# First HGRN tile loaded, turned and given its levels between retention's pieces, in the memory of tokens already projected

## What is computed

```python
def step(state, inp):                     # retention
    scores = jnp.einsum('bqhd,bkhd->bhqk', qc, kc) * decay
    intra = jnp.einsum('bhqk,bkhe->bqhe', scores, vc)
    cross = jnp.einsum('bqhd,bhde->bqhe', qc, state) * q_decay[None, :, :, None]
...
def step(state, inp):                     # HGRN2
    b = jnp.cumsum(lfc, axis=1)
    diff = b[:, :, None] - b[:, None, :]
    w = jnp.where(causal[None, :, :, None, None], jnp.exp(jnp.minimum(diff, 0.0)), 0.0)
    attn = jnp.einsum('bihd,bjhd,bijhd->bhij', qc, kc, w)
    intra = jnp.einsum('bhij,bjhe->bihe', attn, vc)
    cross = jnp.einsum('bihd,bhde->bihe', qc * jnp.exp(b), state)
```

## Time and profile before

| | |
|---|---|
| median of 3 runs | 3606.19 us (3604.67 to 3606.43) |
| profiled execution | 3605.24 us, span 3603.1 us |
| PE busy | 3480.9 us, 97% |
| DVE busy | 2816.3 us, 78% |
| mean granted clock of TensorE | 0.981 |

### The profile page before, as it was taken

How to read it: one execution, slowest core, us unless ns; L and a number is a source line. 1 busy time by engine, 2 the same in 40 slices (tenths; PEclk the granted TensorE clock), 3 DMA queues, 4 the chain that set the end, 5 groups by cost and what they waited for, 6 DMA issues and landing times.

```text
span 3603.1 us, 71005 instructions
## 1 busy us (share of the span) xinstructions
PE 3480.9 (97%) x27042; PEld 2525.5 (70%) x27042; DVE 2816.3 (78%) x5663; ACT 1266.9 (35%) x3545; POOL 520.6 (14%) x798
## 2 busy tenths in 40 slices
PE   7999999999999997999999999999999999989998
PEld 6887888888864565555578878887888445555554
DVE  4666678647988998999955766884598799989996
ACT  3422333334431122444453133333344212234443
POOL 0110000100010355000000000001000115620000
PEclk9999999999999997999999999999999999979999
DMA  7443121322234335233432132214323333433332
GB/s 249 153 160 110 61 80 52 113 87 83 77 106 128 118 115 180 90 107 123 138 123 78 72 99 67 74 49 129 95 72 115 95 111 121 143 137 107 106 114 83
DMA packets 248304, 389.39 MB, mean 108 GB/s; under 512 B 30592, under 2 KB 176224, under 8 KB 247840
## 3 DMA queue, kind: packets, MB, share of 16 engines
q1 hardware_dynamic: 178560, 230.04, 20.6%
q0 software_dynamic: 39968, 122.30, 9.0%
q10 hardware_dynamic: 29440, 32.51, 2.9%
HBM read 264.42 MB, written 122.25 MB: 107 GB/s over the span
## 4 chain that ended last, share of the span: by engine, by line
PE 85%; DVE 10%; issue 2%; DMA 1%; ACT 1%; SPq 0%; DVEq 0%; POOL 0%; ACTq 0%; POOLq 0%
PE ps L1257 35%; PE ps L1665 14%; PE ps L1305 9%; PE ps L1448 5%; PE ps L1430 4%; PE ps L1417 3%; PE ps L1421 2%; PE ps L1618 2%; DVE e_t L2410 2%; PE ps L1580 2%; PE ps L1377 1%; PE ps L1483 1%; PE ps L1643 1%; PE ps L1232 1%; PE ps L1317 1%
## 5 line engine op out<-in xcount | busy, mean ns | idle before, releaser
L1257 PE MATMUL ps<-w_sb,s_t 128*128 128x256 f32 x3456 | 825.8, 382 | 7.4 <-DVE s_t L2337 3.7
L1257 PEld LDWEIGHTS ps<-w_sb,s_t 128*128 128x128 f32 x3456 | 628.0, 190 | 95.3 <-issue 13.0
L1257 PE MATMUL ps<-w_sb,hT 128*128 128x256 f32 x2592 | 635.2, 384 | 5.0 <-ACT hT L1816 2.3
L1665 PE MATMUL ps<-wo_sb,mT 128*128 128x512 f32 x1152 | 536.7, 606 | 2.6 <-ACT mT L2069 2.6
L1305 PE MATMUL ps<-w_sb,hT 128*128 128x512 f32 x1152 | 528.0, 601 | 0.5 <-issue 0.5
L1257 PEld LDWEIGHTS ps<-w_sb,hT 128*128 128x128 f32 x2592 | 473.5, 191 | 74.7 <-issue 11.8
L2315 DVE TENSOR_TENSOR row_t<-ps,p_t 128x256 f32<-128x256 f32 x324 | 136.9, 422 | 349.9 <-PE ps L1257 348.5
L1305 PEld LDWEIGHTS ps<-w_sb,hT 128*128 128x128 f32 x1152 | 207.8, 190 | 213.5 <-issue 209.0
L1665 PEld LDWEIGHTS ps<-wo_sb,mT 128*128 128x128 f32 x1152 | 206.8, 191 | 208.1 <-issue 197.8
L1056 POOL DMA_DIRECT2D projected<-row_t x216 | 117.9, 546 | 1441.4 <-DVE row_t L2400 865.6
L1839 ACT ACTIVATE p_t<-ps 128x256 f32<-128x256 f32 x324 | 124.0, 383 | 534.8 <-PE ps L1257 532.4
(11 more groups left out here) (266 smaller groups left out, 5801.9 us busy)
## 6 DMA issues: line engine op xcount, KB each, us to landing
projected<-row_t POOLq DMA_DIRECT2D x288, 256.0 KB, 2.5
w_sb<-in_w_in ACTq DMA_DIRECT2D x40, 512.0 KB, 5.1
hg_raw<-projected SPq DMA_DIRECT2D x72, 256.0 KB, 4.2
out_streams<-y_t POOLq DMA_DIRECT2D x36, 512.0 KB, 4.8
wa<-in_w_ada SPq DMA_DIRECT2D x10, 1536.0 KB, 7.3
hg_braw<-projected SPq DMA_DIRECT2D x108, 128.0 KB, 2.4
hg_raw<-projected SPq DMA_DIRECT2D x36, 384.0 KB, 3.3
mx_t<-mixed SPq DMA_DIRECT2D x36, 384.0 KB, 5.8
```

What stands on the lines that cost most here:

```text
L1257: mm = nc.tensor.matmul(ps[:, (u.run + k) % 2, 0:HB], x[:, c], w_blk[:, at[w], c * HB:(c + 1) * HB], start=opens and c == 0, stop=(c == KH ...
L1665: mm = nc.tensor.matmul(ps[:, 6 + g, :], mT[:, t % 2, k, :], wo_sb[:, k, g * GRP:(g + 1) * GRP], start=(k == 0), stop=(k == KC - 1))
```

## The change

`hT` is laid out by tiles (`[P, NT, KC, P]`), the tile t at place `NT - 1 - t`, so that the tiles that are projected first lie at its start. HGRN's buffers are cut out of one tensor over the same memory, with the buffers of even tiles in the first half and those of odd tiles in the second. The first half is free once piece (7, 9) is through; SP and POOL wait for that (`hg_room` and its like), SP in slot 19, POOL in slot 20, and then load tile 0 of HGRN and the tables, and clear `hg_d`. PE turns the decays, the queries and the keys of tile 0 in slots 21, 22 and 23, into PSUM bank 2, which `turn_ret` uses too: it waits for `ret.xT_ready` before, and the next `turn_ret` for `bank_taken`. ACT takes them in the same slots. DVE makes one level in each of slots 24 to 30, after all else in the slot, and the edges and keys in slot 31. Tile 1 is loaded, turned and taken where it was.

Left out below are the same change of the index of `hT` at five other places, and unchanged lines.

```diff
@@ -192,6 +192,11 @@
+def place_of(t):
...
+    return NT - 1 - t
@@ -215,6 +220,10 @@
+TURN_AT = 21
+LEVEL_AT = 24
+HG_PARTS = ("decays", "x", "keys")
@@ -371,11 +380,10 @@
-TURN_BANKS, O_BANK = (0, 1), 2
...
-HT_END = KC * NT * P
+TURN_BANKS, O_BANK, RET_BANK = (0, 1), 2, 2
...
+PLACE_N = KC * NT * P
 BLOCKS_AT = 18104
-HG_CORE = 14 * GW + P + 2 * P + 4 * GW + 4 + 12 * P + 16 * P + 8 * LEVELS * P + 8 * P + 128 + (SLOTS + 1) * 64
@@ -460,9 +468,9 @@
     with ExitStack() as s:
-        hT = sb(s, "hT", [P, KC, NT * P])
...
-        wa_early = hT[:, :, :].rearrange("p k n -> p (k n)").rearrange("p (c k n) -> p c k n", k=KC, n=3 * P)
+        hT = sb(s, "hT", [P, NT, KC, P])
...
+        wa_early = hT[:, :, :, :].rearrange("p t k n -> p (t k n)").rearrange("p (c k n) -> p c k n", k=KC, n=3 * P)
@@ -546,20 +554,33 @@
     with ExitStack() as s:
-        hg.raw = sb(s, "hg_raw", [P, 2, 7 * GW])
-        past = sb(s, "past", [P, P])
-        hg.sf = sb(s, "hg_sf", [P, 2, P])
-        hg.ed = sb(s, "hg_ed", [P, 2, GW])
-        hg.kd = sb(s, "hg_kd", [P, 2, GW])
-        hg.total = sb(s, "hg_total", [P, 2, 2])
-        hg.xT = sb(s, "hg_xT", [P, 2, 6, P])
-        hg.d = sb(s, "hg_d", [P, 2, 4, 2 * P])
-        hg.q = sb(s, "hg_q", [P, 2, LEVELS, 2, P])
-        hg.k = sb(s, "hg_k", [P, 2, LEVELS, 2, P])
-        hg.qx = sb(s, "hg_qx", [P, 2, 2, 2, P])
-        hg.tc = sb(s, "hg_tc", [P, 2, 64])
-        keep = sb(s, "keep", [P, SLOTS + 1, 64])
-        sb(s, "w_sb_first", [P, HT_END + KC * GRP - HG_CORE])
+        core = sb(s, "hg_core", [P, 2, PLACE_N // 2])
...
+        def both(at, *dims):
+            part = core[:, :, at:at + int(np.prod(dims))]
+            if len(dims) == 1:
+                return part
+            if len(dims) == 2:
+                return part.rearrange("p b (x n) -> p b x n", n=dims[1])
+            return part.rearrange("p b (x y n) -> p b x y n", y=dims[1], n=dims[2])
...
+        def single(at, n):
+            return core[:, 0, at:at + n]
...
+        hg.raw = both(0, 7 * GW)
+        hg.ed = both(7 * GW, GW)
+        hg.kd = both(8 * GW, GW)
+        hg.xT = both(9 * GW, 6, P)
+        hg.d = both(12 * GW, 4, 2 * P)
+        hg.q = both(16 * GW, LEVELS, 2, P)
+        hg.k = both(23 * GW, LEVELS, 2, P)
+        hg.qx = both(30 * GW, 2, 2, P)
+        hg.total = both(32 * GW, 2)
+        past = single(32 * GW + 8, P)
+        hg.sf = single(32 * GW + 8 + P, 2 * P).rearrange("p (c n) -> p c n", c=2)
+        hg.tc = single(32 * GW + 8 + 3 * P, P).rearrange("p (h n) -> p h n", h=2)
+        keep = single(32 * GW + 8 + 4 * P, (SLOTS + 1) * 64).rearrange("p (s n) -> p s n", n=64)
+        sb(s, "w_sb_first", [P, KC * GRP])
@@ -659,6 +680,9 @@
+    def turn_bank(key):
+        return RET_BANK if key[1] == 0 and key[0] in HG_PARTS else TURN_BANKS[TURNS[(0,) + key] % 2]
@@ -932,6 +956,9 @@
+            def hg_room(eng):
+                eng.wait_ge(proj_done, PIECES[l, 7, place_of(PLACE_N // 2 // D_MODEL - 1)].run + 1)
@@ -978,17 +1005,19 @@
                     load_ret_values(m - FORE + 1)
+                if m == TURN_AT - 2:
+                    hg_room(sp)
+                    load_hg_keys(0)
+                    load_hg_values(0)
+                    sp.dma_start(past[:, :], cols("after")).then_inc(hg.s_in, 16)
+                    sp.dma_start(keep[:, :, :].rearrange("p s n -> p (s n)"), cols("keep")).then_inc(hg.s_in, 16)
+                    for g, src in enumerate(state_ap(st_hgrn, l, 0)):
+                        sp.dma_start(hg.sf[:, 1, g * HD:(g + 1) * HD], src).then_inc(hg.s_in, 16)
...
                     sp.wait_ge(proj_done, last.run + 1)
-                    load_hg_keys(0)
-                    sp.dma_start(past[:, :], cols("after")).then_inc(hg.s_in, 16)
-                    sp.dma_start(keep[:, :, :].rearrange("p s n -> p (s n)"), cols("keep")).then_inc(hg.s_in, 16)
                     load_hg_keys(1)
-                    load_hg_values(0)
                     load_hg_values(1)
-                    for g, src in enumerate(state_ap(st_hgrn, l, 0)):
-                        sp.dma_start(hg.sf[:, 1, g * HD:(g + 1) * HD], src).then_inc(hg.s_in, 16)
@@ -1183,8 +1212,10 @@
                     store_piece(*REST_AT[m - 1])
+                if m == TURN_AT - 1:
+                    pool.wait_ge(proj_done, PIECES[l, 7, place_of(PLACE_N // 2 // D_MODEL - 1)].run + 1)
+                    clear_decays(0)
                 if m == REST_END + 1:
-                    clear_decays(0)
@@ -1302,7 +1333,7 @@
                     for k in range(KC):
-                        mm = nc.tensor.matmul(ps[:, p.bank, :], hT[:, k, t * P:(t + 1) * P], w_sb[:, g % 2, k, :],
+                        mm = nc.tensor.matmul(ps[:, p.bank, :], hT[:, place_of(t), k, :], w_sb[:, g % 2, k, :],
@@ -1516,6 +1547,9 @@
                     pe.wait_ge(ret.bs_ready, l * NT + NT - 1)
+                part = j + FORE - 3 - TURN_AT
+                if 0 <= part < len(HG_PARTS):
+                    pe.wait_ge(bank_taken, TURNS[l, HG_PARTS[part], 0] + 1)
@@ -1572,20 +1606,28 @@
                 n = TURNS[(l,) + key]
-                bank = TURN_BANKS[n % 2]
-                need(pe, bank_taken, n - 1)
+                bank = turn_bank(key)
+                need(pe, bank_taken, n if key[1] == 0 and key[0] in HG_PARTS else n - 1)
...
-            def turn_hg(t):
+            def turn_decays(t):
...
+            def turn_queries(t):
...
+                x = hg.raw[:, t % 2]
...
+            def turn_hg(t):
+                turn_decays(t)
+                turn_queries(t)
@@ -1697,13 +1739,18 @@
                 fill(2 * (more and m > 0))
-                if m == REST_END + 1:
+                if 0 <= m - TURN_AT < len(HG_PARTS):
+                    pe.wait_ge(ret.xT_ready, l * NT + j + 3)
+                if m == TURN_AT:
+                    turn_decays(0)
+                if m == TURN_AT + 1:
+                    turn_queries(0)
+                if m == TURN_AT + 2:
                     pe.wait_ge(hg.s_in, 64 * (l + 1))
+                    turn_keys(0)
+                if m == REST_END + 2:
...
                         bank_out(pe, PIECES[(l,) + PLAIN_ORDER["rest"][-n]])
-                    turn_hg(0)
-                    turn_keys(0)
-                if m == REST_END + 2:
@@ -2043,7 +2090,7 @@
                 act.wait_ge(bank_turned, n + 1)
-                return ps[:, TURN_BANKS[n % 2], :]
+                return ps[:, turn_bank(key), :]
@@ -2131,10 +2178,16 @@
                     bounds_ln(*REST_AT[m])
-                if m in (REST_END + 1, REST_END + 2):
-                    take_decays(m - REST_END - 1)
-                    take_x(m - REST_END - 1)
-                    take_keys(m - REST_END - 1)
+                if m == TURN_AT:
+                    take_decays(0)
+                if m == TURN_AT + 1:
+                    take_x(0)
+                if m == TURN_AT + 2:
+                    take_keys(0)
+                if m == REST_END + 2:
+                    take_decays(1)
+                    take_x(1)
+                    take_keys(1)
@@ -2883,11 +2936,9 @@
                     nc.vector.memset(hg.sf[:, 0, :], 0.0).then_inc(hg.clear, 1)
-                    for lv in range(0, 4):
-                        level_hg(0, lv)
-                if m == REST_END + 2:
-                    for lv in range(4, LEVELS):
-                        level_hg(0, lv)
+                if 0 <= m - LEVEL_AT < LEVELS:
+                    level_hg(0, m - LEVEL_AT)
+                if m == LEVEL_AT + LEVELS:
...
                 if m == BACK_SLOTS - 1:
```

More of the change, by code:

```diff
@@ L1263, in own @@
                     def own(t, kh):
-                        return hT[:, kh * KH:(kh + 1) * KH, t * P:(t + 1) * P]
+                        return hT[:, place_of(t), kh * KH:(kh + 1) * KH, :]
                     new = i == 0
@@ L1815, in modulated @@
                 for k in range(0, 4):
-                    last = nc.scalar.activation(hT[:, k, t * P:(t + 1) * P], ps[:, 2 + 2 * b, k * P:(k + 1) * P],
+                    last = nc.scalar.activation(hT[:, place_of(t), k, :], ps[:, 2 + 2 * b, k * P:(k + 1) * P],
                                                 ACT.Identity, scale=mod[:, d, KC + k, c:c + 1], bias=mod[:, d, k, c:c + 1])
@@ L2294, in modulated @@
                 for k in range(4, KC):
-                    last = nc.vector.tensor_scalar(hT[:, k, t * P:(t + 1) * P], ps[:, 3 + 2 * b, (k - 4) * P:(k - 3) * P],
+                    last = nc.vector.tensor_scalar(hT[:, place_of(t), k, :], ps[:, 3 + 2 * b, (k - 4) * P:(k - 3) * P],
                                                    mod[:, d, KC + k, c:c + 1], mod[:, d, k, c:c + 1], ALU.mult, ALU.add)
```

## The result

The changed kernel takes 3623.51 us (median of 4 runs, 3621.96 to 3626.11) against 3606.31 for the kernel before (4 runs, 3604.67 to 3607.93). The recorded ratio is 1.0050, with a 95% interval of 1.0038 to 1.0063; the two medians alone give 1.0048. It is slower by 17.2 us. The forecast was 3608, the range ended at 3621.

A forecast was written before the change was run, and what follows sets the result against it. PE was taken to bound the slots with pieces; after slot 31 PE and DVE take turns. Per layer +2.9 + 9 - 11 = +0.9, two layers +1.8: 3608 us, range 3590 to 3621.

The forecast's parts named there:

- an exchange: Whole kernel: what DVE loses to the pieces it gets back in the tail; 3608 us, chance 40%.
- Places in memory, POOL's clearing, SP's loads: New index of `hT`, `hg_d` clearing in slot 20, seven transfers thirteen slots earlier: claimed to cost nothing on the path.
- PE and ACT, slots 21 to 23: PE's turns of tile 0 where PE is full, +1.9, and waiting for ACT's copy, +1.0: +2.9 us a layer.
- DVE, slots 24 to 31: Levels made beside POOL's rotation: three group 6 slots at 3 us each, 9 a layer, ends 0 to 13.
- the lead: DVE's `ret_p` is ready 2.3 us before PE takes it up; this was to pay for slot 24's level.
- The caught case: Group 6 slots: POOL's rotation holds the level's later operations and L2408 waits too; 15.2 us, 4.4 over PE's pace.
- the uncaught 1.5: Group 6 slots: the level gets in ahead of POOL's rotation, only L2733 waits; 12.3 us, 1.5 over PE's pace.
- The tail: Slot 31's `ret_p` to slot 34: 31.9 us become 19.5 at full or 25.3 at half clock; 11.5 saved a layer.
- less 0.5 for the store of an earlier tile: Tail: DVE waits for a store that has less time, taking 0.5 us off the 11.5 saved, leaving 11.
- The rotation catches the level: Slower rival, 28%: three group 6 slots at 4.4 us, tail saves 9.5; +6.6 a layer, 3619 us.
- DVE's holds give way: Faster rival, 28%: a later DVE meets less of POOL's rotation, PE never waits; -7.1 us a layer, 3592.
- The loads or the memory come late: Rival, 4%: SP or PE waits in slots 19 to 23, retention's loads behind it; about 3612 us.

## Why the prediction was wrong

The forecast was an exchange, +0.9 us a layer. Measured is some +8.5 a layer. By the steps of the prediction:

- *Places in memory, POOL's clearing, SP's loads*: cost nothing, as said. The new places alone: 3605.59 against 3605.56.
- *PE and ACT, slots 21 to 23*: forecast +2.9, measured +1.5 (the first mark with the levels back in the tail; on PE the slots take 0.44, 0.44 and 0.65 more). PE did not wait for ACT's copy, +1.0 in the forecast.
- *DVE, slots 24 to 31*: forecast 9, with 0 to 13 as its ends; measured 14.1. **This is the first step that failed, a size and not a mechanism.** Slot 24 was to be paid out of the lead, and was, but for 0.7. The caught case was worked out as 15.2 us from `ret_p` to `ret_p`, 4.4 over PE's pace; measured are 15.0, 15.0 and 15.6, and for PE 3.7, 5.3 and 4.3 over. I put 3 for each of these slots, between the uncaught 1.5 and the caught 4.4, though the one row that bore on the race showed DVE losing it. All three were caught, in both layers. Of the 18 such slots in the three kernels that keep the level there (the change and the two with the load on ACT's queue) one escaped, a slot 28, and took 11.3 us.
- *The tail*: forecast 11.5 saved before the store; measured 11.0 and 11.3. The sum is right out of two errors: from `ret_p` to `ret_p` of slot 32 it took 7.9 and not 10.1 (PE's turns no longer lie there, and POOL's hold did not come), and the rest took 13.0, in part at half clock (L1585 at 1.94 and 1.81 us in slots 32 and 33), where 9.4 at full and 15.2 at half clock had been worked out.
- *"less 0.5 for the store of an earlier tile"*: measured some 4 a layer. **This is the second step that failed**: the smaller one in microseconds (3.5 off, against 5.1 for the levels), but the one whose mechanism the prediction didn't have. I looked for what would be late next only up to slot 34. The store does come late (DVE waits 2.32 us for it, 0.73 before), but the price is that of loads under way with it: the 4 MB of output weights now run across HGRN's first tiles, and retention's last gate values and the keys of tile 2 wait for them.

With the measured terms the sum closes: 1.5 + 14.1 - 11.0 + 4 = 8.6 a layer, 17.2 for two, the difference of the medians. That it does so to the tenth is luck: the terms come from one pair of executions, whose spans are 20.9 us apart, and each is good to about half a microsecond.

Of the rivals, "The rotation catches the level" is the one that happened. Its caught slots are shown by the timelines and by the kernel that puts the level ahead of the store: the same levels, 7.8 us a layer less. Its price of 13.2 a layer is close to that of the runs (14.0). Its sum of 3619 was short since it took nothing for what follows slot 34. ("It decides from 3.9 us a slot on, at 9.5 saved" is a slip: at 9.5 saved the two layers pass 3613.4 from 3.4 us a slot on, and 3.9 belongs to 11 saved.) "DVE's holds give way" is refuted: L2733's hold went away when DVE came later, but it was handed to L2842 and L2461, 3.8 us for 1.65. "The loads or the memory come late" was looked for in slots 19 to 23 and didn't happen there; loads did come late, 14 slots further on. Of the signs I named, the pairs grew from slot 26 on (25.75 for 22.0, where I said by about 3, and over 26 for this rival), L2842 took over 1 us in slots 26, 28 and 30, and slot 31's `ret_p` to slot 34's centring took 20.9 us. L1585 at 1.00 us in slots 32 to 34 held for slot 34 only. PE's waits were not where I had put them: up to slot 31 it waits 0.5 us a layer at L1585 for `ret_p` and 5.7 at L1336 for `row_t`, the next piece's gates, which DVE makes behind the held level.

The Trainium skill ("SBUF — State Buffer", section "SBUF: two separate sides") has DVE and GpSimd share an exclusive lock, held by whoever starts first for the whole instruction. That they exclude each other is what the rows show. The order agrees in one case and not in the other. In slot 30 DVE's queries are listed 0.09 us ahead of POOL's key product, which POOL starts after an idle wait; DVE keeps its pace and POOL's operation is the longer one, 0.80 us instead of 0.61:

```profile
1393.23 0.75 DVE L2765 TENSOR_TENSOR ret_qd<-ret_xT,ret_dec 128x256 f32<-128x256 f32 x2
...
1393.66 0.80 POOL L1185 TENSOR_TENSOR ret_kd<-ret_x,ret_dec 128x256 f32<-128x256 f32 x1 [2.75 <-PE ps L1514]
```

But L2842 is listed from 1371.69 and POOL's rotation, which follows the issue of a store without a pause, from 1371.91, and it is L2842 that takes 3.15 us. Start times on POOL are the rough ones of the profile, so whether POOL had the lock before its listed start or the rule fails there stays open. By the rule and the listed times the three slots would have cost 1.5 each, 4.5; they cost 13.3.

## What to carry to other kernels

Where DVE and POOL work on SBUF side by side, price a DVE instruction by the place at which it falls against POOL's chain, and look for the instruction that lets POOL start: work set right behind it is held for the whole chain (15.0 us a slot), the same work ahead of it (12.3), or in the slot whose chain is over, costs little more than itself. And when a stage is shortened, follow the big transfers whose issue isn't shortened with it into the next stage, and only then write down the gain.

## What the runs showed of the hardware

- A DVE operation that the profile lists 0.22 us ahead of POOL's vector operation, while POOL was issuing a transfer, is held: 3.15 us for one that takes 0.42. It is not let in between the first three of POOL's rotation operations (L1173, L1179 twice), only at the fourth (it ends at 1374.84, the fourth is listed from 1374.63). The three such holds of layer 1 took 3.15, 3.15 and 3.26 us. Ahead of POOL's key product (L1185), which POOL starts after an idle wait, it is the other way round: two DVE operations of 0.75 us together, the second listed 0.09 us ahead of it, take no longer, and POOL's takes 0.80 for 0.61.
- DVE operations that read PSUM aren't held: in the kernel with the level ahead of the store, L2466 and L2784 (both `<-ps`) take 0.42 us each at 1371.63 and 1371.97, in the middle of POOL's L1173, and L2786, which reads and writes SBUF alone, is held by 1.1 right behind them. The reciprocal isn't held either, though it works on SBUF alone: in slot 28 of the same kernel L2463 takes 3.35 us from 1356.55, beside POOL's rotation from 1357.33 to 1361.34, and all 36 of this width show that time in the kernel before.
- The load of 4 MB took 14.2 us in the kernel before and 15.1 in the kernel after, and 14.7 and 15.6 from ACT's queue, and loads beside it were late, from another queue too: HGRN's 256 KB took 12.5 us and the gate rows' 512 KB 11.2 with the 4 MB on ACT's queue in slot 34, and 5.7 and 4.7 with the 4 MB in slot 33.
- The same idle time of PE was followed by either clock: after 2.87 us at 1352.74 the granted clock stayed at 1.00, after 2.86 us at 1378.50 it was 0.51 for 3.4 us.
